# Expert rows summed from behind query group 3: two pairs of rows behind each of groups 3 to 6, ScalarE weighing ahead of the groups' copies

## The reference

```python
q = (xb @ w_q).reshape(128, 8, 2, 128)              # 8 heads, two halves
s = einsum('thpd,hpnd->thpn', q, sub_keys)          # 128 sub-keys a half
s_top, i_top = top_k(s, 16)
cand = s_top[:, :, 0, :, None] + s_top[:, :, 1, None, :]
best, pos = top_k(cand, 16)                         # 16 experts a head
expert = take_along_axis(cand_idx, pos)
g = softmax(best)
act = gelu(einsum('td,thkd->thk', xb, u[expert]))   # u: 16384 x 1024
out = einsum('thk,thkd->td', g * act, v[expert])    # v: 16384 x 1024
```

## Time and profile before

| | us |
|---|---|
| median of 3 runs | 1243.74 (1242.19 to 1243.96) |
| the profiled execution's own time | 1244.28 |
| its span, first to last instruction | 1242.5 |
| TensorE busy | 1094.6 (88%) |
| VectorE busy | 802.4 (65%) |
| ScalarE busy | 494.1 (40%) |
| gathers (queue 0): 268.45 MB | 52.1% of the DMA engines' span |
| mean granted TensorE clock | 0.954 |

### The profile page before, as it was taken

How to read it: one execution, slowest core, us unless ns; L and a number is a source line. 1 busy time by engine, 2 the same in 40 slices (tenths; PEclk the granted TensorE clock), 3 DMA queues, 4 the chain that set the end, 5 groups by cost and what they waited for, 6 DMA issues and landing times.

```text
span 1242.5 us, 13686 instructions
## 1 busy us (share of the span) xinstructions
PE 1094.6 (88%) x4964; PEld 741.5 (60%) x4964; DVE 802.4 (65%) x1717; ACT 494.1 (40%) x1052; POOL 295.2 (24%) x313
## 2 busy tenths in 40 slices
PE   9999999998978867788398686877999999999997
PEld 9888887654433323233143232324988988888886
DVE  6587656556766677656875677454776655756574
ACT  5566323224223333242242323323477343574433
POOL 1044103243354333434152543420001000000001
PEclk9999999998989888988699798999999999999999
DMA  5553269899999999999999999997344333443622
GB/s 210 191 182 136 85 203 375 333 421 421 421 408 422 422 421 422 420 422 421 416 422 422 420 422 420 422 422 300 137 170 140 108 131 137 160 174 136 237 75 111
DMA packets 61844, 364.01 MB, mean 293 GB/s; under 512 B 6848, under 2 KB 17360, under 8 KB 20304
## 3 DMA queue, kind: packets, MB, share of 16 engines
q0 software_dynamic: 36864, 268.45, 52.1%
q1 hardware_dynamic: 24448, 94.48, 21.6%
q10 hardware_dynamic: 464, 0.20, 0.1%
HBM read 361.01 MB, written 2.10 MB: 292 GB/s over the span
## 4 chain that ended last, share of the span: by engine, by line
PE 61%; DMA 22%; DVE 8%; issue 4%; POOL 2%; ACT 2%; DVEq 0%; POOLq 0%; ACTq 0%
PE ps L2001 19%; PE ps L2180 17%; DMA big<-in_uv,big 15%; PE ps L1967 10%; DMA ring<-in_uv,big 8%; PE ps L1928 5%; PE ps L2052 2%; DVE lo L1331 1%; PE ps L2115 1%; DVE big L1575 1%; PE ps L1894 1%; POOL big L805 1%; ACT hi L883 1%; POOL ring L805 1%; PE ps L2408 0%
## 5 line engine op out<-in xcount | busy, mean ns | idle before, releaser
L2180 PE MATMUL ps<-big 128*128 128x512 f32 x540 | 262.9, 633 | 91.4 <-ACT big L1038 91.4
L2180 PEld LDWEIGHTS ps<-big 128*128 128x128 f32 x540 | 107.1, 202 | 236.5 <-issue 126.4
L1575 DVE CUSTOM_DVE_ANT_0 big<-big,ps 128x1024 f32<-128x1024 f32 x135 | 163.0, 1220 | 110.4 <-DMA big<-in_uv,big 108.9
L2001 PE MATMUL ps<-hi,x 128*128 128x512 f32 x704 | 226.1, 395 | 1.2 <-DVE lo L1331 1.0
L1331 DVE TENSOR_TENSOR lo<-raw,hi 128x2048 fp32r<-128x2048 f32 x60 | 139.8, 2332 | 75.7 <-ACT hi L883 75.4
L2180 PE MATMUL ps<-ring,big 128*128 128x512 f32 x356 | 169.2, 614 | 20.5 <-ACT big L1038 20.5
L805 POOL DMA_INDIRECT big<-in_uv,big x135 | 129.8, 961 | 223.3 <-PE ps L2180 165.9
L1575 DVE CUSTOM_DVE_ANT_0 ring<-ring,ps 128x1024 f32<-128x1024 f32 x89 | 107.6, 1220 | 79.4 <-DMA ring<-in_uv,big 79.4
L2001 PEld LDWEIGHTS ps<-hi,x 128*128 128x128 f32 x704 | 133.0, 189 | 30.2 <-issue 2.6
L883 ACT ACTIVATE hi<-raw 128x2048 fp32r<-128x2048 f32 x60 | 114.7, 1911 | 71.5 <-PE ps L2001 42.5
L1030 ACT ACTIVATE big<-big 128x2 f32<-128x2 f32 x129 | 25.9, 201 | 284.5 <-DVE big L1575 281.4
(11 more groups left out here) (373 smaller groups left out, 1362.0 us busy)
## 6 DMA issues: line engine op xcount, KB each, us to landing
raw<-in_pieces SPq DMA_DIRECT2D x61, 1024.0 KB, 4.8
ring<-in_peer_w_q SPq DMA_DIRECT2D x8, 1024.0 KB, 6.7
big<-in_up SPq DMA_DIRECT2D x4, 2048.0 KB, 8.7
big<-in_uv,big POOLq DMA_INDIRECT x135
ring<-in_w_mem_kv SPq DMA_DIRECT2D x2, 1024.0 KB, 13.9
ring<-in_uv,big POOLq DMA_INDIRECT x89
resid<-in_x SPq DMA_DIRECT2D x2, 512.0 KB, 4.6
raw<-in_pieces SPq DMA_DIRECT2D x2, 512.0 KB, 9.3
```

What stands on the lines that cost most here:

```text
L1575: ins = dve.tensor_tensor_reduce(out=row, in0=row, in1=hn_ps[n], scale=1.0, scalar=0.0, op0=ALU.mult, op1=ALU.add, accum_out=dots[:, n, s: ...
L2001: ins = pe.matmul(o, a, b[:, c], start=(s == 0 and c == 0 and k == 0), stop=(s == 1 and c == HALF - 1 and k == 2))
L2180: ins = pe.matmul(ps[:, 4 + 2 * n + half, :], diag[:, s % DIAGS], row_home[home_of[k]][:, D + half * TILE:D + (half + 1) * TILE], start=(s ...
```

## The change

`FIRST_ROW`: ring2, actT, query0 and keys open for rows 26 to 29 in place of 20 to 23. TensorE: two pairs behind each of groups 3 to 6 (pairs 0 to 7) in place of 4 to 6 (pairs 0 to 5); from pair 8 on behind the last scores. ScalarE: pair 0 is weighed behind the first exponentials (ahead of the copy of group 3), pair 1 behind the scores' copy of step 3, and then for each of i = 4, 5, 6 one pair ahead of the copy of group i and one behind the scores' copy. VectorE: the first softmax comes behind two dots in place of four.

```diff
--- before.py
+++ after.py
@@ -392,7 +392,7 @@
         row_home["ring0"], row_home["ring1"] = ring_half[0], ring_half[1]
         row_home["mkv"] = sqtmp.rearrange("p n d -> p (n d)")
 
-        FIRST_ROW = {"early0": 0, "early1": 0, "early2": 0, "early3": 0, "ring5": 4, "query1": 5, "mixT": 6, "ring3": 7, "ring4": 8, "ring2": 20, "actT": 21, "query0": 22, "keys": 23,
+        FIRST_ROW = {"early0": 0, "early1": 0, "early2": 0, "early3": 0, "ring5": 4, "query1": 5, "mixT": 6, "ring3": 7, "ring4": 8, "ring2": 26, "actT": 27, "query0": 28, "keys": 29,
                      "memT": 56, "ring0": 56, "ring1": 57, "mkv": 62}
         WEIGHTS_IN_MIXT = range(7, 48)
         LAST_ROWS = 8
@@ -1055,18 +1055,19 @@
             act.wait_ge(group_done, group_no["wq00"] + 1)
             out_tile_query(1).then_inc(group_out, 1)
             for i in range(1, PH):
+                if 4 <= i < PH - 1:
+                    weigh(2 * i - 6)
                 out_query(i)
                 if i == 1:
                     out_tile_scores(1)
+                    out_scores(1)
                 if i == 2:
                     exponentials(0)
+                    weigh(0)
                 if i >= 3:
                     out_scores(i - 1)
-                    if i < PH - 1:
-                        weigh(2 * i - 6)
-                        weigh(2 * i - 5)
-                elif i < 2:
-                    out_scores(i)
+                if 3 <= i < PH - 1:
+                    weigh(2 * i - 5)
             out_scores(PH - 1)
             for b in range(2 * PH - 8, BATCHES):
                 weigh(b)
@@ -1592,10 +1593,11 @@
                     dve.wait_ge(gain_loaded_then_used, 17)
                 if j == NT * PH - 1:
                     scale_rows(0)
-                dot_rows(first, first + 4)
+                ahead = 2 if j == 0 else 4
+                dot_rows(first, first + ahead)
                 if j % 2 == 0:
                     softmax(j // 2)
-                dot_rows(first + 4, first + 8)
+                dot_rows(first + ahead, first + 8)
                 if j + 2 < NT * PH:
                     search_head(j + 2)
                 if j == PH + 1:
@@ -2190,11 +2192,11 @@
                     key_scores(1)
                 elif i > 2:
                     key_scores(i - 1)
-                if 4 <= i < PH - 1:
-                    weighted_rows(2 * i - 8)
-                    weighted_rows(2 * i - 7)
+                if 3 <= i < PH - 1:
+                    weighted_rows(2 * i - 6)
+                    weighted_rows(2 * i - 5)
             key_scores(PH - 1)
-            for b in range(2 * PH - 10, BATCHES):
+            for b in range(2 * PH - 8, BATCHES):
                 weighted_rows(b)
                 if 8 <= b < 24:
                     memory(2 * b, 2 * b + 2)
```

## The result

The changed kernel takes 1250.01 us (median of 5 runs, 1249.78 to 1251.39), the kernel before 1243.74 (1242.19 to 1244.95). The ratio is 1.006, with a 95% interval of 1.0049 to 1.0071; the two medians by themselves lie 0.50% apart. In a later set it was 1248.79 against 1242.70, 1.0049 (1.0037 to 1.0061). By the medians that is 6.1 to 6.3 us, where I had forecast 1.9, and both times above my range, which ended at 1248.6.

A forecast was written before the change was run, and what follows sets the result against it. Row transfers at 421 GB/s bound the kernel. No work added, first hole moved (-0.1 to +0.2), row 24 later by 1.9: 1246.2 us against the profiled 1244.28, 1245.6 against the median 1243.74; range 1241.6 to 1248.6.

The forecast's parts named there:

- the first gap: Transfers' hole of 3.95 us before row 13 moves from 228 to 216, before row 8; -0.1 to +0.2 us.
- No stall at pair 0: TensorE, pair 0: diagonals ready at 202.9, needed at 203.90; the 1.28 us table load need not add.
- The 2.0 us wait of pair 8: TensorE stands still from 264.5 to 266.5, as weighing pair 8 stands behind ScalarE's copy of the last scores.
- row 24 tied to pair 8: Row 24 takes ring4 behind pair 8 and goes out at 270.45 us, where it was 261.31.
- the 5.62 of row 13: Issue-to-landing time behind an empty queue, applied to row 24: landing 276.05 us, 1.9 later, nothing added behind it.
- slower rival: Hole before row 24, 269 to 272.6, counts in bytes as all engines idle: +3.9 us, 1247.6; chance 0.22.
- A: Experiments' theory: the end moves as row 24's bytes start later; shift is its issue after row 0 less 80.67 us.
- B: The prediction's theory: only row 24's landing counts, since slow engines catch up in the gap; 1.9 us forecast.
- My own sign for it: Rows 24 to 35 landing more than 2.485 us apart would decide for the slower rival.
- the fall at the new wait: TensorE's clock falls at pair 8's 2.0 us wait: pair takes 6.2, +2.5 us, 1248.1; chance 0.05.
- its gate at 347.9: End of the memory product lets row 56 out at about 347.9 us, before its turn at 349.7.
- the faster rival: TensorE sets the pace up to row 56; pause between rows 55 and 63 could go: 3.0 us, 1240.8; chance 0.13.

The follow-up runs named there:

- the repeated run: The changed kernel once more, with no edit, on another chip beside the kernel before: 1248.79 us, ratio 1.0049.
- pair 8 weighed first: The changed kernel with pair 8 weighed ahead of the copy of the last scores instead of behind it: 1244.93 us, ratio to the kernel before 1.0017.
- 8 fillings: The changed kernel with 8 small unused matmuls on TensorE between the last scores and pair 8: 1247.25 us, ratio to the kernel before 1.0033.
- 16 fillings: The changed kernel with 16 small unused matmuls on TensorE between the last scores and pair 8: 1249.56 us, ratio to the kernel before 1.0054.
- homes from 24: The changed kernel with ring2, actT, query0 and keys opened for rows 24 to 27 instead of 26 to 29: 1243.68 us, ratio to the kernel before 1.0007.
- homes from 20: The changed kernel with ring2, actT, query0 and keys opened for rows 20 to 23, as in the kernel before: 1249.56 us, ratio 1.0053.
- row 8's home: The changed kernel with ring4 opened for row 12 instead of row 8, so row 8 waits for pair 0: 1248.44 us, ratio to the kernel before 1.0039.
- both homes: The changed kernel with ring4 opened for row 12 and ring2, actT, query0, keys for rows 24 to 27: 1240.29 us, ratio to the kernel before 0.9971.
- both, pair 8 first: As both homes, with pair 8 also weighed ahead of the copy of the last scores: 1240.04 us, ratio to the kernel before 0.9974.
- ScalarE's part alone: The kernel before with only the change's ScalarE order and early VectorE softmax; TensorE's order and homes as before: 1242.92 us, ratio 0.9998.

## Why the prediction was wrong, point by point

**Right.** What bounds the kernel, and that the end moves with the rows: 384.1 us behind row 255's dot in both. That the first gap is not closed but moved from 228 to 216, because row 8 waits for query 4 behind two more pairs (218.49; 217.9 forecast plus the 0.55 by which the run was late). No stall at pair 0: the table load ran at 197.87, ahead of its activation's wait. Row 23 as before (271.37; 272.0 forecast). The 2.0 us wait of pair 8 behind the last scores' copy (2.02), and row 24 tied to pair 8. By the experiments each of these counts as I had it in the changed kernel: the first gap by itself nothing, the wait only through row 24.

**Wrong: what row 24's lateness costs.** The step was "it takes the 5.62 of row 13: landing 276.05. That is 1.9 us later", with the slow engines working through the gap. What the runs show is the rule that I had as the slower rival at 0.22, A's: the kernel pays about the time for which the queues stood empty in bytes. In the repeated run B gives +1.9 (84.58 + 5.62 - 88.31) and 4.37 came. With A in the sum my own issue time gives 84.57 - 80.67 = +3.9.
A's short formula looks at row 24 alone. The windows' GB/s can be summed in full: a stretch of the trace has lost its length times (1 - GB/s / 421), 421 being the full rate. In us, by stretches counted after row 0, and beside it how much later than before row 79's dot came, A's shift where row 24 or 20 waits for its gate, and row 255's dot:

| | 20 to 60 | 60 to 95 | 95 to 200 | sum, less before | row 79, less before | A | row 255, less before |
|---|---|---|---|---|---|---|---|
| before | 6.9 | 0.2 | 1.0 | | | | |
| changed | 6.9 | 5.9 | 0.1 | +4.9 | +5.06 | +5.6 | +5.57 |
| changed again | 6.8 | 4.6 | 0.9 | +4.2 | +4.42 | +3.9 | +4.37 |
| pair 8 weighed first | 6.8 | 2.5 | -0.1 | +1.1 | +1.32 | +2.0 | +1.95 |
| 8 fillings | 6.8 | 5.6 | 0.3 | +4.6 | +4.60 | +4.6 | +5.17 |
| 16 fillings | 6.7 | 5.7 | 1.9 | +6.2 | +6.02 | +5.2 | +6.59 |
| homes from 24 | 6.5 | 0.5 | -0.1 | -1.2 | -0.24 | | +0.45 |
| homes from 20 | 6.8 | 5.7 | 0.2 | +4.7 | +4.82 | +5.3 | +5.42 |
| row 8's home | 1.1 | 11.8 | 0.0 | +4.9 | +5.07 | +5.6 | +5.65 |
| both homes | 1.1 | 2.5 | 1.3 | -3.1 | -2.68 | | -2.08 |
| both, pair 8 first | 1.1 | 2.2 | 0.0 | -4.8 | -4.92 | | -4.34 |
| ScalarE's part alone | 6.8 | 0.2 | 1.3 | +0.3 | +0.43 | | +0.41 |

The empty time and the shift of the rows go together to within about 0.4 us in all runs but one (homes from 24, 1.0). The first gap costs 6.9 us before and 6.9 changed, so it did only move; the second is the loss. Beside this A's short formula is right to about 0.6, and in the run with 16 fillings 1.4 short; where it fits to a few hundredths (2.0 against 1.95) that is luck, since at row 79 the same run stands at 1.32.
The landing price itself was not what failed: a row that goes out into an empty queue landed 5.45, 5.62 and 5.85 us behind its issue. What failed is that nothing would be added behind it. By row 43 the seven runs with a late row 24 or 20 are 1.2 to 2.0 us later than that row's landing makes them (5.62 us behind its issue where VectorE doesn't show it). The surplus comes in no fixed place: in the changed kernel as one step of 1.53 us (rows 37 to 38), in the repeated run 1.1 us by row 27 and the rest later. My own sign for it, rows 24 to 35 more than 2.485 apart, would have missed it in the changed kernel, where rows 27 to 37 keep the pace to the hundredth (24.85 us for ten). I took the 2.485 us between rows 23 and 55 as proof that nothing else could be lost. The trace of before had the same kind of step in front of them, seven rows behind its own gap; these are the dots of rows 19 and 20, 4.01 us apart:

```profile
260.24 1.22 DVE L1575 CUSTOM_DVE_ANT_0 big<-big,ps 128x1024 f32<-128x1024 f32 x1 [1.25 <-DMA big<-in_uv,big]
264.25 1.22 DVE L1575 CUSTOM_DVE_ANT_0 ring<-ring,ps 128x1024 f32<-128x1024 f32 x1 [2.77 <-DMA ring<-in_uv,big]
```

Why the surplus comes, by slow engines whose lag returns or otherwise, no run here shows.

**Wrong: the clock.** I gave the fall at the new wait 0.05 and cited a longer idle stretch (2.5 us and more before 791.01) that had left the clock alone. It fell in the profiles of the changed kernel, of the homes at 20 and at 24, of row 8's home and of both homes: five of the six with that wait unfilled, and not in the sixth. Between the two runs of the changed kernel it made pair 8 1.7 us longer (5.23 against 3.54, where I had 6.2 for the lower level), row 24's issue 1.7 later and the end 1.2. Slower rival and clock came together; I had priced each alone.

**Missed: row 56.** I had its gate at 347.9, with 1.8 us to spare, and "no gap of note" between rows 55 and 63 before. But the kernel before already lost about 1.0 us of bytes around this gate (the third stretch of the table). In the first run of the changed kernel row 56 went out at 352.77, and as the rows were later too, 354.5 would have done (row 55 at 357.88, a row's pace of 2.485 behind it, less 5.85 from issue to landing): next to nothing was lost (0.1 in the table), and rows 55 and 63 only 21.80 us apart in place of 22.84. Where the rows were a little less late or the gate later, the loss was there again: 0.9 in the repeated run, 1.9 with 16 fillings, 1.3 with both homes changed. With 16 fillings this explains 0.9 of the 1.4 over A. The 0.5 and 0.6 over A of the repeated run and of 8 fillings it does not explain, since the kernel before pays as much there or more; they are near what can be read at all.

**A slip in the range.** Half way from 1245.6 to the faster rival's 1240.8 is 1243.2, not 1241.6. The miss was on the other side.

**The price of row 24's landing.** The 4.4 us estimated from the Trainium skill ("DMA: Bandwidth & Descriptors", section "Anatomy of one DMA — SWDGE (gpsimd) path") would have put row 24's landing 1.2 us earlier than I did. The traces do not agree with the page's figure: the three direct rows here have 5.62 (row 13 before), 5.85 (row 24 with row 8's home changed) and 5.45 us (row 20 with the homes from 20) from issue to VectorE's start.

## What to carry to other kernels

When a stream of transfers bounds the kernel, ask for each buffer which event opens it, and follow the tightest one to the end: a gap that is closed early only moves, unless the next gate moves with it. Here an order that cost 0.5% became 0.3% faster than the kernel before with five numbers changed (which row first uses which buffer). The kernel before with its own order and row 8's home changed was not run, so how much of the 0.3% needs the new order is open. And price an empty queue by the bytes it does not move, not by when the next transfer lands.

## What the runs showed of the hardware

TensorE's granted clock after one and the same 2.02 us of idle time fell to its lower level (1.2 GHz) in five profiles and stayed at 2.4 GHz in a sixth; pair 8 took 5.23 and 3.54 us in the two profiles of the changed kernel. A similar thing happens long before: in the kernel before and the changed one 48 matmuls starting at about 55 us took 12.77 and 12.76 us with a granted clock down to 0.59 and 0.53 in windows of 2.5 us, in the run with the homes at 24 the same ones took 11.16 at 1.00. Over all twelve profiles this parts the issue times of row 0: 183.72 to 184.23 us in the five where the clock stayed at 1.00 between 55 and 60 us, 185.42 to 186.43 in the seven where it fell. So most of the 2.7 us by which row 0's issue differs goes with this one event (the 48 matmuls alone make 1.6), ahead of all that was edited. How much of the spread between unprofiled executions it makes was not measured.

A row's landing lags its bytes, and behind an empty queue part of that lag was missing at first and came back within some 20 rows: 1.2 to 2.0 us by row 43 in the seven runs. What the single steps in full stream are (1.53 us at row 38 in the changed kernel, 1.52 at row 20 in the kernel before, 1.55 at row 30 with 16 fillings), and which of the 16 engines carries them, the profile's means over the engines can't show; this stays open.
